# A thirteenth group of seven products in the convolution's columns, and the values' last pieces moved behind the squares

## The reference

```python
h = rms_norm(x, norm_g[l])
proj = jnp.einsum('bsd,dn->bsn', h, w_in[l])
... bz, cqkv, cb, ca, cz = jnp.split(proj, split_points, axis=-1)
qkv = jax.nn.silu(causal_depthwise_conv(cqkv, d_conv_w[l]))     # 4 taps, 3 x 1024 channels
q_c, k_c, v_c = jnp.split(qkv, 3, axis=-1)
q_c = l2_normalize(q_c...); k_c = l2_normalize(k_c...)
g = -jnp.exp(d_a_log) * jax.nn.softplus(ca + d_dt_bias)
o_c = gated_delta_chunked(q_c, k_c, v_c, g, beta)
...
y = jnp.concatenate([y_a, y_b, y_c], axis=-1)
x = x + jnp.einsum('bsm,md->bsd', y, w_out[l])
```

## Time and profile before

| | us |
|---|---|
| median of three runs (lowest, highest) | 1515.87 (1515.27, 1516.86) |
| profiled execution | 1517.49 |
| its span | 1515.7 |

### The profile page before, as it was taken

One profiled execution on the slowest core, in us unless ns is written; L12 is line 12 of the kernel. 1 busy time (PEld: TensorE's weight loads), 2 busy tenths in 40 slices (PEclk: granted clock), 3 DMA queues, 4 the chain that ended last, 5 costly groups with the idle time before them and its releaser, 6 DMA issues.

```text
span 1515.7 us, 19030 instructions
## 1 busy us (share of the span) xinstructions
PE 1511.2 (100%) x6906; PEld 1251.9 (83%) x6906; DVE 1138.1 (75%) x1714; ACT 813.0 (54%) x1084; POOL 360.2 (24%) x606
## 2 busy tenths in 40 slices
PE   9999999999999999999999999999999999999999
PEld 7888888888888887888878888888888888888887
DVE  6889899757759855576579676676557779988885
ACT  6766656587533444554545545544345645555553
POOL 9040131330230040126520254344400112000000
DMA  9887687986788785558865787898875667686766
GB/s 292 279 237 220 198 248 205 233 250 195 223 247 263 242 221 165 159 183 267 254 201 167 231 250 199 246 276 235 250 244 174 189 214 235 195 237 207 220 214 163
DMA packets 207438, 338.32 MB, mean 223 GB/s; under 512 B 53065, under 2 KB 60536, under 8 KB 207088
## 3 DMA queue, kind: packets, MB, share of 16 engines
q1 hardware_dynamic: 184784, 288.66, 62.5%
q0 software_dynamic: 22512, 48.42, 12.1%
q10 hardware_dynamic: 48, 0.02, 0.0%
HBM read 312.81 MB, written 27.68 MB: 225 GB/s over the span
## 4 chain that ended last, share of the span: by engine, by line
PE 94%; DVE 4%; DMA 1%; ACT 1%; issue 1%; ACTq 0%; DVEq 0%
PE acc L1275 25%; PE acc L1278 25%; PE acc L1277 25%; PE mix L1275 2%; PE mix L1278 2%; PE mix L1277 2%; PE mix L1293 1%; PE mix L1291 1%; PE mix L1292 1%; PE acc L1291 1%; PE acc L1293 1%; PE acc L1292 1%; DVE w_lo L1994 1%; PE mix L1384 1%; PE mix L1467 1%
## 5 line engine op out<-in xcount | busy, mean ns | idle before, releaser
L1994 DVE TENSOR_TENSOR w_lo<-w_raw,w_hi 128x1024 fp32r<-128x1024 f32 (+1 forms) x505 | 606.8, 1215 | 251.2 <-ACT w_hi L1612 245.7
L1612 ACT ACTIVATE w_hi<-w_raw 128x1024 fp32r<-128x1024 f32 (+1 forms) x505 | 525.6, 1050 | 388.6 <-PE acc L1278 284.1
L1275 PE MATMUL acc<-w_hi,op_hi 128*128 128x512 f32 (+1 forms) x1636 | 644.0, 394 | 0.3 <-DVE w_lo L1994 0.3
L1278 PE MATMUL acc<-w_hi,op_lo 128*128 128x512 f32 (+1 forms) x1636 | 637.1, 389 | 0.0
L1277 PE MATMUL acc<-w_lo,op_hi 128*128 128x512 f32 (+1 forms) x1636 | 637.0, 389 | 0.0
L1275 PEld LDWEIGHTS acc<-w_hi,op_hi 128*128 128x128 f32 x1636 | 307.5, 188 | 64.8 <-issue 1.3
L1278 PEld LDWEIGHTS acc<-w_hi,op_lo 128*128 128x128 f32 x1636 | 307.3, 188 | 64.2
L1277 PEld LDWEIGHTS acc<-w_lo,op_hi 128*128 128x128 f32 x1636 | 307.5, 188 | 61.7
L979 POOL DMA_DIRECT2D conv_dram<-y x48 | 30.7, 699 | 166.6 <-DVE y L2086 119.5
L1275 PE MATMUL mix<-w_hi,op_hi 128*128 128x512 f32 x162 | 62.9, 388 | 0.0
L1277 PE MATMUL mix<-w_lo,op_hi 128*128 128x512 f32 x162 | 62.9, 388 | 0.0
(11 more groups left out here) (558 smaller groups left out, 1761.9 us busy)
## 6 DMA issues: line engine op xcount, KB each, us to landing
w_raw<-in_w_in_dram SPq DMA_DIRECT2D x367, 512.0 KB, 4.6
w_raw<-in_w_out_dram SPq DMA_DIRECT2D x128, 512.0 KB, 4.4
w_raw<-in_w_in_dram SPq DMA_DIRECT2D x16, 384.0 KB, 3.8
w_raw<-in_a_wuq_dram SPq DMA_DIRECT2D x12, 512.0 KB, 5.4
out_dram<-in_x_dram POOLq DMA_DIRECT2D x7, 512.0 KB, 6.8
conv_dram<-y POOLq DMA_DIRECT2D x48, 64.0 KB, 4.0
y<-conv_dram POOLq DMA_DIRECT2D x48, 64.0 KB, 4.4
w_raw<-in_a_wuqi_dram SPq DMA_DIRECT2D x6, 512.0 KB, 4.4
```

What stands on the lines that cost most here:

```text
L1275: nc.tensor.matmul(o, hi[:, kt, tok], hv[:, i, n0:n1], start=(kt == (kts if late else blk["kts"])[0]), stop=False)
L1278: last_mm = nc.tensor.matmul(o, lo[:, kt, tok], hv[:, i, n0:n1], start=False, stop=(kt == blk["kts"][-1]))
L1612: func(split_ap(w_hi, c), w_raw[:, c % RAW_BUFS, 0:n], ACT.Copy).then_inc(hi_ready, 1)
L1994: vec.tensor_tensor(split_ap(w_lo, c), w_raw[:, c % RAW_BUFS, 0:n], split_ap(w_hi, c).bitcast(F32), ALU.subtract).then_inc(lo_ready, 1)
```

## The change

The second pair gets a seventh group (contraction pair 6), and x's sums with it; `CONV_ORDER` and `PAIR_SLOTS` are rewritten, `CONV_SLOTS` as well. The values' last three pieces (9, 10, 11) stand in slots 110 to 136, behind the start of the squares, whose wait asks for eight finished pieces in place of twelve. The values' way through DRAM stands later in POOL's queue, behind the loads for the triangular solve, and their turns stand in slots 195 and 197.

```diff
-SEVEN = [[0, 1, 2, 3, 4, 5], [0, 1, 2, 3, 4, 5],
+SEVEN = [[0, 1, 2, 3, 4, 5], [0, 1, 2, 3, 4, 5, 6],
...
-CONV_ORDER = ["12S1111S11S1122S22S22S1222", "12S11S11S11S11S22S12222222"]
-X_S = [0, 1, 2, 3, 4, 5]
-CONV_SLOTS = [(33, 34, 35), (35, 37, 39), (38, 43, 45), (46, 51, 53), (72, 78, 79), (75, 87, 89),
-              (80, 91, 91), (82, 94, 94), (97, 99, 100), (99, 104, 105), (104, 105, 107), (106, 108, 109)]
+CONV_ORDER = ["1211S11S11S1122S22S22S1222", "12S11S11S11S12S2222S22S12"]
+X_S = [0, 1, 2, 3, 4, 5, 6]
+CONV_SLOTS = [(31, 40, 41), (31, 43, 45), (42, 53, 55), (49, 57, 59), (71, 77, 79), (77, 81, 83),
+              (77, 85, 86), (86, 93, 95), (101, 103, 103), (110, 127, 129), (127, 130, 132), (131, 134, 136)]
 CSQ_FROM = 110
-PAIR_SLOTS = [(59, 60, 62, 63), (88, 89, 89, 97)]
+V_FROM = 195
+PAIR_SLOTS = [(59, 61, 61, 64), (93, 94, 94, 97)]
...
-    weave(g_end + 1, [("vd", 0), ("vd", 1)], 2)
+    weave(V_FROM, [("vd", 0), ("vd", 1)], 2)
...
-            pool.wait_ge(conv_ready, 12)
-            for hg in range(2):
...
             wait_read(pool, "cn", 7)
             clear_corners(1)
...
+            pool.wait_ge(conv_ready, 12)
+            for hg in range(2):
...
+                pool.wait_ge(v_kept, 16 * 4 * (M + hg + 1))
...
-                act.wait_ge(conv_ready, 12)
+                act.wait_ge(conv_ready, 8)
```

More of the change, by code:

```diff
@@ L1046, in _ @@
                                ).then_inc(lane_left_loaded, 16)
+            pool.wait_ge(conv_ready, 12)
+            for hg in range(2):
+                for i in range(4):
+                    pool.dma_start(v_dram[hg].rearrange("a f j i b -> i a (f j) b")[i],
+                                   v_heads(hg)[32 * i:32 * i + 32].rearrange("p (f b) -> p f b", b=32)
+                                   ).then_inc(v_kept, 16)
+                pool.wait_ge(v_kept, 16 * 4 * (M + hg + 1))
+                for j in range(4):
+                    pool.dma_start(v_heads(hg)[32 * j:32 * j + 32].rearrange("p (f c) -> p f c", c=P),
+                                   v_dram[hg][:, :, j].rearrange("a f i b -> a f (i b)")).then_inc(v_moved[hg], 16)
             pool.wait_ge(v_kept, 16 * 8 * M)
```

## The result

The changed kernel takes 1520.37 us (median of ten, 1519.24 to 1520.92); the kernel before, run beside it ten times, 1515.99. The ratio is 1.0028, 95% interval 1.0019 to 1.0036: slower by 4.4 us, between 2.9 and 5.5. The forecast was 1517.9, so the time lies in the range and on the slower side, and the likeliest case (no change, 67%) did not come. The profiled execution of the changed kernel took 1520.92 with a span of 1519.1.

What follows compares the result with a forecast made beforehand. TensorE, busy 1511.2 of 1515.7 us, was taken as the bound, with time coming in where weights' low parts end late. -0.68 + 0 + 0.65 + 1.7 + 0.3 = +2.0 on 1515.87 gave 1517.9; range 1514.9 to 1520.8.

Steps and rivals of the forecast that it cites:

- the likeliest case: Whole kernel: a difference under 0.2% (3.03 us), counted as no change; 67%.
- The 13th group: Second pair's added group: three matmuls fewer on TensorE at 0.228 us each, -0.68 us.
- Slots 29 to 65: Convolution pieces 0 to 3 move to later slots; smallest margin about 1 us at slot 47, cost 0.
- Slots 71 to 97: Second pair: VectorE 0.15 us late at slot 85 and 0.5 at slot 89; +0.65, between 0 and 1.3.
- Slots 99 to 110: Three pieces leave these slots; nothing waited on TensorE, so nothing is gained and only risk goes: 0.
- Slots 127 to 146: Pieces 9 to 11 ahead of splits: 1.1 at slot 131, 0.5 at 138, 0.1 at 140; +1.7, 1.1 to 2.7 (late weights).
- The six loads: ScalarE, values' SiLUs among exponentials: six more table loads, 7.7 us beside its idle time; cost 0 by themselves.
- rival 3: Each of the six loads followed by a 1.3 us pause, on the path at slots 134, 136, 140: +5.9 us, 4%.
- The values' way: Values' transfers and turns moved, slots 158 to 197: contention with the solve's loads, +0.3 us, between 0 and 1.5.
- The signs: TensorE's waits grow from 1.7 to about 4 us, largest at slot 131 (0.8 to 1.2), then slot 138; six more loads.
- rival 2: Slots 131 to 140: ScalarE's and VectorE's queues hold each other, TensorE halts 2.7 us and more; +3.1 to +6, 27%.
- Rival 1: Margins hold, only three matmuls and perhaps a halt go: -0.7 to -1.2 us, 1514.9 to 1516.3, 18%.

Runs made afterwards that it cites:

- e1: The changed kernel with piece 8 of the convolution three slots later (slots 104, 105, 107): 1518.96 us, ratio 1.0015 to the kernel before.
- e2: The kernel before with the values' part alone (pieces 9 to 11 in slots 110 to 136, transfers and turns late): 1519.41 us, ratio 1.0019.
- f3: The changed kernel with piece 8 in slots 104, 105, 106 and piece 9 in slots 104, 107, 108: 1516.35 us, ratio 0.9997 to the kernel before.
- f1: e1 with the SiLUs of pieces 9 and 10 moved to slot 136, beside that of piece 11: 1517.76 us, ratio 1.0006 to the kernel before.
- e4: The changed kernel with pieces 9 to 11 in VectorE's pauses, slots 110 to 122: 1522.73 us, ratio 1.0046 to the kernel before.
- g2: The changed kernel with piece 6's products and SiLU in slots 90 and 92, not 85 and 86: 1520.63 us, ratio 1.0027 to the kernel before.

## Why the prediction was right and wrong

- **The bound and the method.** Right: the time followed TensorE's margins, the granted clock was 1.00 in both windows above, and behind slot 142 nothing moved.
- **The 13th group, -0.68.** Right: slots 84 to 94 give -0.68 where nothing waits (e1).
- **Slots 29 to 65, 0.** Right: no loss, and the margin at slot 47 is 0.9 where I had about 1.
- **Slots 71 to 97, +0.65.** The size was right, one assumption under it wrong. I forecast 0.15 at slot 85 and 0.5 at slot 89; the trace has 0.08 and 0.66. (By my own terms slot 85 is 236.05 - 235.95 = 0.10; the sum stays 0.65, since slot 89 then comes 0.05 later.) Over the seven kernels with piece 6 in slot 85 slot 89 lost 0, 0.1, 0.3 to 0.4, 0.6 (three times, the changed kernel's 0.66 among them) and 1.0, some 0.5 in the mean. But I took the halt at 230.37 for fixed; it was in no other trace, and the walk started from 204.03, a time that a late weight had set. A walk from one execution carries that one's lateness along; here it is 0.75 and 1.6 us at the same slot for the same order.
- **Slots 99 to 110, 0.** This step failed. I wrote that three pieces leave and that what goes is only risk, at no cost. What did not leave is piece 8, and its turn waits for a block whose way through DRAM starts at the accumulators' emptying, which `PAIR_SLOTS` had moved by five slots. I followed the work on VectorE and not the data it waits for. What stands behind it, the products and the SiLU with the split of slot 107, came late with it. 1.28 in this trace, 2.1 and 2.2 in two others; e1 takes it away.
- **Slots 127 to 146, +1.7.** The mechanism and the first term right: 1.1 forecast at slot 131, 1.09 found, with and without the group (e2), and gone with piece 9 (f3). Slot 134: margin 0.2 forecast, no loss. Slot 138 was mis-sized: 0.5 forecast, 1.35 found (1.0 to 1.35 in four traces), and slots 139 to 141 took 0.34 for 0.1. The high part of slot 136 began at 380.37. My 378.9, put off by the 0.64 by which TensorE and VectorE ran later at slot 130, is 379.5; 0.7 of the other 0.8 is the wait of the high part before it for weights, which I had kept as the high end (2.7) and not in the sum. The whole is 2.8: the high end.
- **The six loads, 0.** Partly wrong. Six there are (25 loads in the trace for 19), 1.28 us each, and the next activation follows at once (377.89 and 379.18). But those ahead of slot 136 are in the chain that makes the loss at 138, as f1 shows in direction. The Trainium skill (page ScalarE: Activation LUTs, What ACT_TABLE_LOAD costs) adds a drain of ~1380 ns behind each; by this trace there is none, 379.18 - 377.89 leaving 0.01 beside the load itself, and rival 3 falls with it.
- **The values' way, +0.3.** Nothing. The high part of slot 158 waited 5.45 us for weights, against the 5.96 of the earlier trace rows, and its margin for TensorE grew from 1.3 to 1.8:

```profile
445.79 1.06 ACT L1613 ACTIVATE w_hi<-w_raw 128x1024 fp32r<-128x1024 f32 x1 [5.45 <-DMA w_raw<-in_w_in_dram]
```

- **The sum.** Forecast +2.0. Found, with the means of the traces where the same place was seen more than once: -0.68, -0.1 ahead of slot 82, +0.5 at slots 85 and 89, +1.85, +1.09, +1.2 at 138 and +0.36 behind: +4.2, and the medians say 4.4. Of the 2.2 that I missed, 1.85 are the turn of piece 8 and 0.95 slots 138 to 141; 0.3 for slot 158, 0.15 at slots 85 to 89 and 0.1 ahead of slot 82 go the other way.
- **The range.** That the time lies in it is in part luck. The term that took it there, piece 8, was in none of its high ends; without that place the sum of the traces is +2.35, near the forecast, and that again because 0.95 missed at slots 138 to 141 meets some 0.55 on the other side.
- **The signs.** The waits grew from 1.7 to 4.9 us, forecast about 4. The one at slot 131 is 1.03, within the 0.8 to 1.2 that I gave, but the longest is that at slot 138 (1.18), which I had put second, and the one of 0.66 at slot 107 I did not have.
- **The rivals.** The time fell where rival 2 put it (1519.0 to 1521.9), with half of its mechanism: slots 131 to 140 lost 1.0 more than the sum had, over weights, loads and queues that wait for each other. The rest, piece 8, has no rival of mine. Rival 1, that the margins hold, is out: TensorE lost time at slots 89, 105 to 107, 131 and 138. (Its lower end should have been 1515.87 - 1.2 = 1514.7 and not 1514.9.)

## What to carry to other kernels

When a step is left where it is and its producer is moved, follow the data: put the time at which the block lands, not the work on the waiting engine, beside the place where it is waited for. A pause of an engine is room only if what ends it is not the other engine that the same work needs (e4); read what ended the pause and how busy that engine is. And in a lag that carries over from slot to slot, the first step put ahead of a thin margin pays for all that follow: taking one piece out gave back both halts (f3).

## What was not expected of the hardware

One order of instructions met margins that differed by up to 1.6 us between executions (0.66, 1.4 and 2.3 at slot 83), with the arrival of weights: a halt of 0.3 us in one trace is no property of a kernel. The first four slots end up to 2 us apart, for the same reason or others that I did not look into. Piece 8's wait for its block at slot 101 cost 1.28, 2.10 and 2.17 us in three traces with the same order around it (the changed kernel, g2, e4).
